# The feed-forward norm's list of work: turning a pair of tiles in the same step as the rounding of the pair before it

## The chip, the cores and the metric

The kernel runs on one core of a Trainium2 chip. The metric is the device time of one execution in microseconds; the times below are medians over runs.

## The reference, cut to what matters

The program computes two transformer blocks on 256 tokens of width 2048. The place of the change is the second half of the first block:

```
h = rmsnorm(x, norm_ffn_g) * (1.0 + scale_f) + shift_f
g, u = split(h @ ffn_w_in)              # 2048 x 2*5632
x = x + gate_f * ((silu(g) * u) @ ffn_w_down)
```

Everything is in float32. A product of float32 matrices is made of three products of rounded parts: weights and activations are each split into a rounded part (hi) and the rest (lo), and hi x hi, hi x lo and lo x hi are summed.

## The kernel before, in words

**Matrix products.** All weights stream from memory in chunks of two 128-row tiles (512 KB for a width of 512). SyncE loads a chunk into one of five raw buffers. ScalarE rounds it into a buffer of WHI (four of them), VectorE writes what is left into WLO, and TensorE then does the chunk's "unit": for both row tiles and both halves of the tokens three matmuls of 512 columns, twelve in all, with a tile of the activations standing in the array. A job is one output width of 512 over all of its chunks. The feed-forward's first job is fg 0, the second fu 0; each has eight units.

**The norm.** Before fg 0 the activations have to be normalized and turned, so that features lie on partitions. There are 16 feature tiles, handled as eight pairs. The parts are: `f_rn` (row sums, and the inverse root on GpSimd), `warm` (16 matmuls on constants), `f_sc` of a pair (VectorE scales the rows of X into XN), `f_T` of a pair (TensorE turns the pair, four transposes, into a PSUM bank; ScalarE multiplies and adds the modulation into hraw), `f_hi` of a pair (ScalarE rounds hraw into H's hi half; VectorE writes the rest into the lo half), and `f_gfb` (GpSimd loads a gain, once pair 7's rest is written). hraw has two places, one for even and one for odd pairs, so the scaling of pair n waits for the rest of pair n - 2. Unit n of fg 0 reads pair n. Each waits for its data by semaphores.

**What sets the order.** The order is made once, when the program is built: `make_timeline` (from line 417) makes one list, and each engine goes through this list and issues its own share of every entry, so the list is the order of every engine's queue. A stage such as "ffn" is a list of steps written out in `stage_steps` (lines 303 to 415). After every unit each running stage moves on by one step. Ahead of a unit, `until(*stat_need(...))` moves the stages on further until the steps that write this unit's pair and the next unit's are in the list (lines 464 to 471 say which step that is). "prep" entries, the conversion of a weight chunk, are put three units ahead of the unit that uses it. At fg 0, which is one of the BORDERS, the needed steps are put ahead of the "prep" of that moment. The stage "ffn" starts after the last unit of the output projection, xo 3.

The functions behind the parts: `f_T` for TensorE at line 1038, for ScalarE at 1551 with `norm_T` at 1376; `f_hi` at 1558 with `norm_hi` at 1387; VectorE's `f_sc` at 2250 and `f_hi` at 2256 with `norm_lo` at 1984; GpSimd's `f_gfb` at 2648. TensorE's `unit` (line 1203) asks `stationary` for pair n with

```
w.wait_ge(h_hi, at("h", s, k // 2))
w.wait_ge(h_lo, at("h", s, k // 2))
```

In rows of the trace, gp<-whi,h and gp<-wlo,h are a unit's matmuls, tp<-cst,xn a turning (line 833), hraw<-tp,modc ScalarE's scaling, h<-hraw its rounding, h<-hraw,h VectorE's rest, whi<-raw and wlo<-raw,whi a weight chunk's conversion, xn<-xs,stat the scaling of X.

Of the kernel before, what the change touches and what calls it, by code (L numbers as in the profile page):

```python
# [302 lines left out]
def stage_steps(sid):  # L303
# [3 lines left out]
    def step(*parts, need=()):  # L307
        return (list(parts), list(need))
# [23 lines left out]
    if kind == "gla":  # L332
        steps = [step(("gla_z", (), 0), ("gla_sc", (8, 0), 1), need=[("evac", "q", 1), ("evac", "k", 1)]), step(("gla_sc", (8, 1), 1))]
        steps += [step(("gla_sum", (p,), 1), need=[("gk", 5)]) for p in range(4)]
        steps += [step(("gla_diff", GLA_ORDER[0], 0)), step(("gla_exp", GLA_ORDER[0], 0))]
        for i, x in enumerate(GLA_ORDER):
            ahead = GLA_ORDER[i + 1:i + 2]
# [14 lines left out]
        (j,) = args  # L352
        return [idle, idle, idle, step(("mt_T", (j, 0), 1)), step(("mt_T", (j, 1), 1))]
    if kind == "ffn":
        steps = []
        for pair in range(8):
            first = [("f_rn", (), 0), ("warm", ("hf", 0), 1), *[("f_sc", (n,), 0) for n in range(4)]] if pair == 0 else []
            ahead = [("f_sc", (n,), 0) for n in (pair + 3, pair + 4) if pair in (1, 3)] + ([("f_gfb", (), 0)] if pair == 7 else [])
            steps += [step(*first, ("f_T", (pair,), 1)), step(*ahead, ("f_hi", (pair,), 0))]
        return steps  # L360
    if kind == "fx":
        (j,) = args
# [22 lines left out]
    if kind == "ret":  # L385
        l, which = args
        steps = []
# [8 lines left out]
    if kind == "diff":  # L396
        (l,) = args
        steps = []
# [5 lines left out]
    if kind == "lend":  # L404
# [3 lines left out]
        steps = []  # L408
# [8 lines left out]
def make_timeline(jobs, units, chunks):  # L417
# [6 lines left out]
    def launch(*sid):  # L424
        active.append([sid, 0, stage_steps(sid)])

    def step():
        for a in list(active):
            sid, i, steps = a
            parts, need = steps[i]  # L430
            if any(x not in done for x in need):
                continue
            for name, args, n in parts:
                got = []
                for _ in range(n):
                    b = rank[0] % 4
                    rank[0] += 1
                    got.append(Use(b, bank_n[b]))
                    bank_n[b] += 1
                uses[(name, *args)] = got  # L440
                line.append((name, args))
            done.add((*sid, i))
            a[1] += 1
            if a[1] == len(steps):
                done.add(sid)
                active.remove(a)
                if sid[0] == "adaf":
                    launch("fnorm", sid[1])
                if sid == ("fnorm", 2):
                    launch("tables")  # L450
                if sid[0] == "lx" and sid[2] == 1:
                    launch("lru", sid[1])
                if sid[0] == "lfirst":
                    done.add(("layer", 0))
                    launch("lres")
                if sid[0] == "lend" and sid[1] == 0:
                    done.add(("layer", 1))
# [8 lines left out]
    def stat_need(job, k):  # L466
        s = job["stat"]
        if s == "h":
            return [("fnorm", k // 4)]
        if s == "hf":  # L470
            return [("ffn", k // 2 * 2 + 1)]
        if s in ("lq", "lk"):
            return [("lat", s[1], 3 + k // 2)]
        if s == "ot":
            return [("pair", k // 2)]
        if s == "mt":
            return [("mt", k // 4, 3 + k % 4 // 2)]
        if s == "a":
            return [("fx", 6 * job["args"][0] + k // 4, 2 + k % 4 // 2)]
        if s == "h0":  # L480
            return [("hx", k // 4, 1 + k % 4 // 2)]
        if s == "h1":
            return [("lend", 0, k // 2)]
        if s == "mx":
            l = job["args"][0]
            if k < 6:
                return [("ret", l, k % 2, 12 + k // 2)]
            return [("diff", l, 10 * (k - 6) + 9)] if k < 10 else [("lg", l, (k - 10) // 3)]
        return []
# [3 lines left out]
    for n, (job, ci) in enumerate(units):  # L493

        if job["name"] in BORDERS and ci == 0:
            for k in job["order"][0:2]:
                for kk in range(job["kn"]):
                    until(*stat_need(job, k + kk))
# [13 lines left out]
        if job["kind"] != "ada":  # L512
# [15 lines left out]
            for k in job["order"][ci:ci + (1 if (job["name"], ci) == (("ymla", 0), 6) else 2)]:  # L528
                for kk in range(job["kn"]):
                    until(*stat_need(job, k + kk))  # L530
# [2223 lines left out]
```

## Time and profile before

| | us |
|---|---|
| median of 3 runs | 2645.58 |
| lowest, highest | 2645.3, 2647.14 |
| the profiled execution, its own time | 2647.02 |
| its span, first to last instruction | 2645.2 |
| busy: TensorE, VectorE, ScalarE, GpSimd | 2556.9, 1699.3, 1282.6, 63.3 |
| mean granted TensorE clock | 0.994 |

Busy time is a union of an engine's instructions, counted over the span. A row of the timeline gives the start, the duration, the engine, the line, the operation with what it writes and reads, how many were merged into it, and in brackets the idle time of the engine before it and what ended that. A merged row's duration covers all of its instructions. In the table by stretches a row gives, for each engine, the busy time and the number of instructions that started in it, and at the end TensorE's granted clock (1.00 is 2.4 GHz), the busy share of the DMA engines and their rate in GB/s.

### The profile page before, as it was taken

The page shows a single profiled execution, that of the slowest core. Times are in us where ns is not written, and L with a number is a line of the kernel's source. Part 1 is how long each engine was busy: PE and PEld are TensorE (multiplying, and loading weights), DVE is VectorE, ACT ScalarE, POOL GpSimd, SP SyncE. Part 2 cuts the span into 40 slices and gives each one's busy share as a digit, 9 for nine tenths or more (in the row PEclk, how much of TensorE's full clock was granted, in tenths as well). Part 3 has the DMA queues.
Part 4 walks back from the last instruction along what each step waited for, and adds up shares of the span by engine and source line. Part 5 has one row for each costly group of instructions (what it writes and reads, how often), then busy time and mean ns, then how long its engine had stood idle before and what let it go on. Part 6 is the DMA issues. An engine that isn't in the chain of part 4 may idle for free.

```text
span 2645.2 us, 33987 instructions
## 1 busy us (share of the span) xinstructions
PE 2556.9 (97%) x12327; PEld 2147.6 (81%) x12327; DVE 1699.3 (64%) x2194; ACT 1282.6 (48%) x1824; POOL 63.3 (2%) x102
## 2 busy tenths in 40 slices
PE   3889999999999999999999999999999999999999
PEld 3888887888887887788888888888888887988887
DVE  5887776776676755566655545565666655676664
ACT  3345455444555444544443444455755545565553
POOL 0000000000000000000000000000000100010000
PEclk9999999999999999999999999999999999999999
DMA  9984665888675765687756666556665465665564
GB/s 363 340 262 152 184 207 183 286 308 269 205 251 192 237 205 180 192 281 252 269 190 192 191 191 190 183 186 182 182 188 175 136 216 148 187 187 176 150 200 135
DMA packets 279921, 555.73 MB, mean 210 GB/s; under 512 B 24287, under 2 KB 45101, under 8 KB 279117
## 3 DMA queue, kind: packets, MB, share of 16 engines
q1 hardware_dynamic: 274048, 541.79, 64.6%
q0 software_dynamic: 3040, 8.69, 1.0%
q10 hardware_dynamic: 2668, 3.09, 0.3%
q8 instruction: 100, 1.64, 0.3%
q14 instruction: 65, 0.52, 0.1%
HBM read 549.83 MB, written 2.10 MB: 209 GB/s over the span
## 4 chain that ended last, share of the span: by engine, by line
PE 90%; DVE 4%; ACT 2%; issue 1%; DMA 1%; SPq 0%; POOL 0%; DVEq 0%; ACTq 0%
PE gp L830 83%; PE tp L830 5%; PE tp L833 2%; DMA raw_first<-in_ada_w_dram 1%; DVE wlo L1884 1%; ACT whi L1270 1%; DVE acc L1890 1%; DVE xs L1884 0%; ACT hraw L1270 0%; SPq L813 0%; DVE stat L2208 0%; ACT sx L1270 0%; DVE sx L1884 0%; DVE yd L1884 0%; ACT h L1270 0%
## 5 line engine op out<-in xcount | busy, mean ns | idle before, releaser
L1884 DVE TENSOR_TENSOR wlo<-raw,whi 128x1024 fp32r<-128x1024 f32 (+1 forms) x830 | 986.1, 1197 | 699.7 <-ACT whi L1270 697.1
L830 PE MATMUL gp<-whi,h 128*128 128x512 f32 (+1 forms) x4352 | 1373.2, 389 | 11.5 <-DVE h L1884 5.5
L1270 ACT ACTIVATE whi<-raw 128x1024 fp32r<-128x1024 f32 (+1 forms) x830 | 851.5, 1037 | 666.6 <-PE gp L830 537.3
L830 PEld LDWEIGHTS gp<-whi,h 128*128 128x128 f32 x4352 | 816.4, 188 | 171.5 <-issue 19.6
L830 PE MATMUL gp<-wlo,h 128*128 128x512 f32 (+1 forms) x2176 | 835.6, 384 | 0.0
L830 PEld LDWEIGHTS gp<-wlo,h 128*128 128x128 f32 x2176 | 410.4, 189 | 72.8 <-issue 1.7
L1890 DVE SCALAR_TENSOR_TENSOR acc<-raw,cact,acc 128x1024 f32<-128x1024 f32 x149 | 190.6, 1279 | 7.7 <-DMA raw<-in_ada_w_dram 7.0
L830 PE MATMUL gp<-whi,ah 128*128 128x512 f32 x352 | 138.0, 392 | 0.0
L830 PE MATMUL gp<-whi,al 128*128 128x512 f32 x352 | 137.1, 390 | 0.0
L830 PE MATMUL gp<-wlo,ah 128*128 128x512 f32 x352 | 137.0, 389 | 0.0
L830 PE MATMUL gp<-h,whi 128*128 128x256 f32 (+1 forms) x528 | 107.2, 300 | 20.7 <-ACT whi L1270 10.7
L830 PEld LDWEIGHTS gp<-h,whi 128*128 128x128 f32 (+1 forms) x528 | 88.5, 202 | 25.5 <-issue 15.9
L830 PE MATMUL gp<-whi,mxh 128*128 128x512 f32 x256 | 99.8, 390 | 0.0
L830 PE MATMUL gp<-whi,mxl 128*128 128x512 f32 x256 | 99.6, 389 | 0.0
L830 PE MATMUL gp<-wlo,mxh 128*128 128x512 f32 x256 | 99.6, 389 | 0.0
L830 PE MATMUL gp<-h,wlo 128*128 128x256 f32 (+1 forms) x272 | 79.8, 293 | 0.0
L830 PEld LDWEIGHTS gp<-whi,al 128*128 128x128 f32 x352 | 66.1, 188 | 13.9
L830 PEld LDWEIGHTS gp<-wlo,ah 128*128 128x128 f32 x352 | 66.1, 188 | 13.4
L830 PEld LDWEIGHTS gp<-whi,ah 128*128 128x128 f32 x352 | 66.1, 188 | 13.5
L2603 POOL TENSOR_TENSOR stat<-stat,cst 128x2 f32<-128x2 f32 (+1 forms) x37 | 30.2, 817 | 1436.9 <-DVE stat L1887 1436.8
L1270 ACT ACT_TABLE_LOAD x44 | 56.5, 1283 | 6.1 <-issue 2.8
L830 PEld LDWEIGHTS gp<-wlo,mxh 128*128 128x128 f32 x256 | 48.1, 188 | 10.0
(331 smaller groups left out, 2594.2 us busy)
## 6 DMA issues: line engine op xcount, KB each, us to landing
raw<-in_w_in_dram SPq DMA_DIRECT2D x310, 512.0 KB, 4.3
raw<-in_ffn_w_in_dram SPq DMA_DIRECT2D x176, 512.0 KB, 4.5
raw<-in_ada_w_dram SPq DMA_DIRECT2D x158, 512.0 KB, 5.0
raw<-in_w_out_dram SPq DMA_DIRECT2D x96, 512.0 KB, 4.4
raw<-in_ffn_w_down_dram SPq DMA_DIRECT2D x88, 512.0 KB, 4.4
raw<-in_w_in_dram SPq DMA_DIRECT2D x64, 384.0 KB, 3.5
raw_first<-in_ada_w_dram SPq DMA_DIRECT2D x34, 512.0 KB, 7.5
raw<-in_gla_wo_dram SPq DMA_DIRECT2D x32, 512.0 KB, 5.7
```

The costliest lines, as they stand in the source:

```text
L830: return e.matmul(o, l, r, start=start, stop=stop)
L833: return e.transpose(o, i, ident[0:n, 0:n])
L1270: return e.activation(o, i, f, **kw)
L1884: return e.tensor_tensor(o, a, b, op)
L1890: return e.scalar_tensor_tensor(out=o, in0=a, scalar=s, in1=b, op0=op0, op1=op1)
L2603: e.tensor_tensor(dst, dst, cst[:, C_HALF:C_HALF + n], ALU.pow).then_inc(pow_out, 1)
```

## The change

The diff has two hunks. The first writes out the steps of the stage "ffn": before, a pair was turned in one step and rounded in the next, 16 steps; now pair 0 is turned in a step of its own, and each of eight further steps rounds a pair and turns the next. In those steps the rounding stands first, then the turning of the next pair, then the scalings of later pairs (pairs 4 and 5 with pair 1, pairs 6 and 7 with pair 3). The second hunk says which step a unit's pair comes from.

```
     if kind == "ffn":
-        steps = []
+        steps = [step(("f_rn", (), 0), ("warm", ("hf", 0), 1), *[("f_sc", (n,), 0) for n in range(4)], ("f_T", (0,), 1))]
         for pair in range(8):
-            first = [("f_rn", (), 0), ("warm", ("hf", 0), 1), *[("f_sc", (n,), 0) for n in range(4)]] if pair == 0 else []
-            ahead = [("f_sc", (n,), 0) for n in (pair + 3, pair + 4) if pair in (1, 3)] + ([("f_gfb", (), 0)] if pair == 7 else [])
-            steps += [step(*first, ("f_T", (pair,), 1)), step(*ahead, ("f_hi", (pair,), 0))]
+            more = [("f_sc", (n,), 0) for n in (pair + 3, pair + 4) if pair in (1, 3)] + ([("f_gfb", (), 0)] if pair == 7 else [])
+            ahead = [("f_T", (pair + 1,), 1)] if pair < 7 else []
+            steps += [step(("f_hi", (pair,), 0), *ahead, *more)]
         return steps
...
         if s == "hf":
-            return [("ffn", k // 2 * 2 + 1)]
+            return [("ffn", k // 2 + 1)]
```

## Rows read from the trace of the kernel before

**Rows 1.** The page: TensorE's busy time; the chain of waits by engine and line

```profile
PE 2556.9 (97%) x12327; PEld 2147.6 (81%) x12327; DVE 1699.3 (64%) x2194; ACT 1282.6 (48%) x1824; POOL 63.3 (2%) x102
...
PE gp L830 83%; PE tp L830 5%; PE tp L833 2%; DMA raw_first<-in_ada_w_dram 1%; DVE wlo L1884 1%; ACT whi L1270 1%; DVE acc L1890 1%; DVE xs L1884 0%; ACT hraw L1270 0%; SPq L813 0%; DVE stat L2208 0%; ACT sx L1270 0%; DVE sx L1884 0%; DVE yd L1884 0%; ACT h L1270 0%
```

**Rows 2.** Stretches from unit to unit; columns as told above

```profile
1048.62:1050.31 1.69, 0.00 (x1) 0.00 (x1) 0.84 (x4) 0.00 (x0) 0.71 (x1) 1.00 0.04 16
1050.31:1051.49 1.18, 1.18 (x8) 0.84 (x8) 1.18 (x6) 0.41 (x1) 0.00 (x0) 1.00 0.00 0
1051.49:1053.64 2.15, 0.00 (x2) 0.03 (x1) 1.18 (x4) 2.12 (x5) 0.00 (x0) 1.00 0.00 0
1053.64:1058.05 4.41, 4.41 (x12) 3.44 (x13) 2.73 (x6) 1.62 (x3) 0.00 (x0) 0.61 0.13 15
1058.05:1058.41 0.36, 0.36 (x6) 0.36 (x4) 0.00 (x0) 0.00 (x0) 0.00 (x0) 1.00 0.36 46
1058.41:1062.86 4.45, 3.44 (x20) 2.68 (x18) 1.83 (x2) 3.46 (x7) 0.00 (x0) 1.00 0.27 103
1062.86:1082.01 19.15, 16.73 (x77) 12.85 (x77) 10.19 (x14) 12.37 (x20) 0.00 (x0) 1.00 0.48 137
1082.01:1084.73 2.72, 2.72 (x12) 2.28 (x13) 1.23 (x1) 1.42 (x2) 1.60 (x3) 1.00 0.81 265
...
1092.89:1713.00 620.11, 620.11 (x2772) 511.98 (x2770) 349.01 (x320) 257.15 (x269) 0.96 (x2) 1.00 0.69 216
```

**Rows 3.** Stretches at the norm ahead of layer 1

```profile
2212.37:2214.19 1.82, 0.00 (x0) 0.00 (x1) 0.98 (x4) 0.00 (x0) 0.71 (x1) 1.00 0.65 228
2214.19:2216.10 1.91, 1.77 (x8) 1.13 (x8) 1.01 (x3) 0.84 (x2) 0.00 (x0) 0.72 0.03 10
...
2216.85:2221.99 5.14, 5.14 (x12) 3.99 (x13) 3.19 (x5) 2.40 (x6) 0.00 (x0) 0.51 0.10 7
2221.99:2225.19 3.20, 3.20 (x17) 2.64 (x16) 1.55 (x3) 1.79 (x3) 0.00 (x0) 1.00 0.34 112
```

**Rows 4.** Timeline from pair 2's turning to its rest; last, scalings ahead of pair 3's rest

```profile
1058.82 1.02 ACT L1270 ACTIVATE hraw<-tp,modc 128x256 f32<-128x256 f32 x2 [3.52 <-issue]
...
1059.73 1.06 ACT L1270 ACTIVATE whi<-raw 128x1024 fp32r<-128x1024 f32 x1
...
1060.68 0.62 ACT L1270 ACTIVATE h<-hraw 128x512 fp32r<-128x512 f32 x1
...
1060.89 1.23 DVE L1884 TENSOR_TENSOR wlo<-raw,whi 128x1024 fp32r<-128x1024 f32 x1 [4.27 <-ACT whi L1270]
...
1062.03 0.68 DVE L1884 TENSOR_TENSOR h<-hraw,h 128x512 fp32r<-128x512 f32 x1
...
1065.10 1.14 DVE L1887 TENSOR_SCALAR xn<-xs,stat 128x256 f32<-128x256 f32 x4
```

**Rows 5.** Timeline ahead of unit 0: VectorE and ScalarE

```profile
1049.64 2.19 DVE L1887 TENSOR_SCALAR xn<-xs,stat 128x256 f32<-128x256 f32 x8 [0.84 <-POOL stat L2603]
...
1052.80 0.69 DVE L1884 TENSOR_TENSOR h<-hraw,h 128x512 fp32r<-128x512 f32 x1 [0.97 <-ACT h L1270]
...
1054.25 1.04 ACT L1270 ACTIVATE whi<-raw 128x1024 fp32r<-128x1024 f32 x1
```

**Rows 6.** The half microsecond before the granted clock falls

```profile
1054.00:1054.50 0.50, 0.50 (x4) 0.41 (x3) 0.50 (x4) 0.50 (x2) 0.00 (x0) 0.99 0.00 0
```

**Rows 7.** Stretches at an idle time in an early stage

```profile
263.00:264.80 1.80, 0.00 (x0) 0.00 (x0) 1.80 (x4) 0.21 (x1) 0.00 (x0) 1.00 0.12 10
264.80:266.00 1.20, 1.14 (x10) 1.15 (x11) 1.20 (x3) 0.00 (x0) 0.00 (x0) 1.00 0.81 215
266.00:269.30 3.30, 3.30 (x14) 2.91 (x13) 2.04 (x2) 3.12 (x4) 0.00 (x0) 0.50 0.47 141
```

**Rows 8.** DMA issues from 1040 to 1100: KB each, median us to landing

```profile
raw<-in_ffn_w_in_dram SPq DMA_DIRECT2D x14, 512.0 KB, 3.9
gfb<-in_final_norm_g_dram POOLq DMA_DIRECT2D x1, 1024.0 KB, 8.2
```

## The prediction

> **What bounds the kernel now.** I read the page first: TensorE is busy 97% of the span and its three lines hold 83, 5 and 2% of the chain of waits [rows 1]. Time is therefore gained only where TensorE stands still or runs slowly, and an edit counts only there. Next I cut the stage of the change into stretches, one per weight chunk ("unit": twelve matmuls of 512 columns), from the first matmul of one to that of another [rows 2]. In that table look at the length of a stretch against TensorE's busy time in it, and at the clock. The stage starts once the sums of squares are in (1048.62) and ends at 1084.73, where the job fg 0 is through and fu 0 begins; from 1092.89 on TensorE is busy for 620.11 of 620.11 us.
>
> Unit 1 with the turning behind it has 4.45, units 2 to 6 together 19.15, unit 7 2.72. What would a unit take if nothing were late? The turning between units 0 and 1 costs TensorE 0.36 (1058.05 to 1058.41) [rows 2]. The same twelve matmuls and a turning in the other norm of this kind, where nothing was late, took 3.20 (2221.99 to 2225.19) [rows 3]. So a unit with a turning costs 3.20, of which 2.84 are its own; unit 7, with none behind it, took 2.72 [rows 2]. Units 1 to 6, five with a turning and unit 6 without, would need 5 x 3.20 + 2.72 = 18.72; they have 23.60, and in the difference of 4.9 TensorE is idle.
>
> Why they are late is seen in one round [rows 4]. TensorE turns pair 2 at 1058.05. ScalarE scales it at 1058.82, converts a weight chunk at 1059.73 (the next thing in its list), rounds the pair at 1060.68; VectorE takes the chunk's rest at 1060.89 and the pair's rest at 1062.03, ending at 1062.71. Unit 2 starts 0.15 later. So 4.66 us pass from the turning to the pair being whole, and TensorE has only unit 1 (2.84) and the next turning to put there. For pair 3 VectorE also has four scalings ahead of the pair's rest, another 1.14 us [rows 4].
>
> **The change, part by part.** *The order.* Units need the same pairs as before, but a pair's rounding and the next pair's turning are one step. Worked through the list by hand: before, the list was T0, hi0, T1, hi1, chunk 3, unit 0, T2, chunk 4, hi2, unit 1, T3, chunk 5, hi3. After it is T0, hi0, T1, hi1, T2, chunk 3, unit 0, hi2, T3, chunk 4, unit 1, hi3, T4, chunk 5, unit 2. No instruction is added or removed: 32 transposes, 16 scalings of XN, 16 of hraw, 8 roundings, 8 rests. Each of T2 to T7 stands one unit earlier on TensorE.
>
> *T2 ahead of unit 0.* TensorE has nothing from 1051.49 to 1053.64, since unit 0 waits for pair 0's rest (1052.80 plus 0.69) [rows 2, 5]. T2 needs the sixth of the eight scalings, done by about 1049.64 + 6 x 0.27 = 1051.3 (0.27 is an eighth of their 2.19). It costs nothing there: 0.6 in a gap of 2.15. Were the gap gone it would cost its 0.36.
>
> *T2 and the chunk on ScalarE.* T2's two scalings (0.91 to the next start) now precede chunk 3, which started at 1054.25 [rows 5]. It starts at 1055.16 and is whole at about 1057.5; unit 3 wants it after 1063. Nothing on TensorE waits. The raw buffer behind it is freed 0.9 later; SP's load of the chunk five further on is issued so much later, and that chunk's conversion waits for unit 4 anyway. VectorE's four scalings for pairs 4 and 5 fall behind pair 1's rest: pair 1 is wanted only after unit 0.
>
> *A later round.* Pair 3 is turned right behind unit 0 in the place of pair 2. With the durations of [rows 4] (0.91, 0.95, then 0.62 on ScalarE, 1.14 and 0.69 on VectorE) it is whole 4.7 after that. It is wanted by unit 3, two units and two turnings later: 0.36 + 3.20 + 3.20 = 6.76. Slack 2.1. For pair 4 the four scalings stand behind the rest of pair 3 and not ahead of it, and have the same slack to go into. ScalarE needs 0.62 + 0.91 + 0.95 = 2.48 per unit and VectorE 1.14 + 0.69 + half of 1.14 = 2.40, both under 3.20. So the waits should all go, and the stage is TensorE's own time. Units 5 to 7 have no turning behind them now.
>
> *The sum without the clock.* From unit 0's start at 1053.64 to 1084.73 are 31.09. After: unit 0 with turning as before 4.77 (4.41 + 0.36), units 1 to 4 with turning 4 x 3.20 = 12.80, then 2.84 + 2.72 + 2.72 = 8.28; together 25.85. Gain 5.24: the 4.9 of waiting, and T2's 0.36, which now lies in a gap.
>
> *The clock.* Unit 0 took 4.41 and not 2.84 because the granted clock, full until 1054.5 [rows 6], has a mean of 0.61 in this stretch [rows 2]: it fell to the lower level, 1.2 in place of 2.4 GHz, 0.8 after unit 0 began and was back at the turning. What came before the fall: two idle times, 1.69 and 2.15, with 1.18 of turning between them. T2 takes about 0.5 off the second: 1.7 idle, 1.7 turning, 1.6 idle. Does the clock still fall? For a fall: elsewhere it fell 1.2 after a single idle time of 1.8 [rows 7], and before the norm of layer 1 it fell with 1.8 idle and then sparse transposes [rows 3]. Against: up to 1051.49 it had stood through an idle 1.69 and 1.18 of turning [rows 2]. Bounds: nothing, or 4.41 - 2.84 = 1.57. I take 1.57, since the piece that held (idle 1.69, turning) is nearest to the new second gap of 1.6 with more turning ahead of it; but it is close. Sum: 5.24 + 1.57 = 6.8.
>
> The Trainium skill (TensorE: Matmul & The Clock Gate, "Part 1: The HAM clock gate") says the gate's observation runs freely and doesn't begin with the kernel, so the same program meets it at another point each run. By that page neither outcome need hold in every execution, the gain would be 5.24 in some and 6.8 in others, and the fall in layer 1 could be shorter or longer after any shift; no single trace here can show it.
>
> That other fall can move for the same kernel time: it cost 5.14 for a first unit against 4.41 here, and 1.91 for the turnings against 1.18 [rows 2, 3], so 1.5 more. I allow 1.5 either way for it in the range.
>
> *Everything behind.* TensorE leaves the stage 6.8 earlier and is full afterwards. The loads: eight chunks of 0.52 MB and the 1.05 MB for GFB now in 24.3 us is 216 GB/s; from 1092.89 to 1713 the same rate, 216, went with a full TensorE [rows 2]. GFB's load took 8.2 us to land [rows 8] and is issued earlier by the gain and a bit more; its reader is the last norm of the block, far behind. Nothing is given back.
>
> **How it stands to the times.** The profiled execution took 2647.02 with a span of 2645.2; the median of three is 2645.58, 1.44 less. Taking 6.8 off gives 2640.2 for the profiled one and 2638.8 for the median, which I predict.
>
> **Rivals.** *A, forecast:* waits gone and clock held: 2638.8. Chance 0.46.
> *B: the clock falls all the same* at unit 0. 5.24 only: 2640.3, or down to 2638.9 if the other fall is the shorter one. For it: the falls of [rows 3, 7], after no longer idle times than are left here. Chance 0.37.
> *C: a new wait comes in.* The 4.7 of a round assumes that ScalarE is free when the turning ends; if each pair still ends late by half of today's excess, 2.6 remain: 2643.0. Against: slack of 2. Chance 0.08.
> *D: the change does nothing,* since the units' needs pull the steps forward and the list comes out nearly as before: 2645.6. Against: by hand the turnings do move. Chance 0.05.
> *E: slower.* Place: SP's ring of five raw buffers. It is emptied faster while GFB's load runs beside it. A chunk is loaded when its buffer's last rest is done and converted four units before use: five units of 2.72 less 2.3 for conversion and rest, 11 us later, with 8 more (three units) in converted chunks. It decides when a load lands after more than 19 us; price, each us beyond, and 5.24 + 5.3 have to be lost: 2651. Against: these loads land in 3.9 and GFB's own in 8.2 [rows 8]. Chance 0.04.
>
> **Numbers.** About 0.2% (5.3 us) is what a measurement of this kernel can tell from no change, and B's gain lies right at it. Faster: 0.46 x 0.9 + 0.37 x 0.55 = 0.62. Slower 0.04, the rest 0.34. Range: A and B with 1.5 for the other fall below A, up to nearly C above: 2636.8 to 2642.6; out are D, E and part of C.
>
> **What would show it.** In the profile after: T2 within 0.2 us of T1's end and before unit 0; unit starts 3.20 apart from unit 1 to unit 5, 2.7 to 2.8 after; no wait of TensorE for the rests of pairs 2 to 7; from unit 0 to fu 0 24.3 (A) or 25.9 (B); the clock row of unit 0 at 1.00 (A) or about 0.6 (B). Wrong if a unit after the first waits for a pair's or chunk's rest, or if the gain at fu 0 is lost by the end of the span.

## The result, and the profile after

| | us |
|---|---|
| changed kernel, median of 7 runs (lowest to highest) | 2637.97 (2635.92 to 2639.63) |
| kernel before, median of 7 runs beside it | 2646.16 (2642.69 to 2647.62) |
| ratio, 95% interval | 0.9969, 0.9957 to 0.998 |
| again, side by side: changed, median of 11 runs; before, median of 18 | 2639.19; 2645.67 |
| ratio, 95% interval | 0.9978, 0.997 to 0.9987 |
| profiled execution after: time, span | 2638.86, 2637.0 |

The kernel became faster by 0.2 to 0.3%, and both intervals lie below 1. In the two comparisons the medians differ by 8.2 and by 6.5 us; the trace says how much of it is the change's.

The changed kernel in stretches that correspond to those of [rows 2] (idle, turning, idle, unit 0, unit 1 with a turning, units 2 to 5, unit 7, and last the whole from unit 0 to fu 0):

```profile
1047.50:1049.19 1.69, 0.01 (x2) 0.01 (x1) 0.84 (x4) 0.00 (x0) 0.71 (x1) 1.00 0.02 8
1049.19:1050.90 1.71, 1.71 (x12) 1.25 (x12) 1.52 (x6) 0.94 (x2) 0.00 (x0) 1.00 0.00 0
1050.90:1052.52 1.62, 0.00 (x1) 0.03 (x1) 0.69 (x1) 1.59 (x4) 0.00 (x0) 1.00 0.00 0
1052.52:1055.37 2.85, 2.85 (x13) 2.28 (x14) 1.94 (x6) 2.82 (x6) 0.00 (x0) 1.00 0.00 0
1055.72:1058.93 3.21, 3.21 (x20) 2.64 (x18) 2.14 (x3) 2.48 (x4) 0.00 (x0) 1.00 0.38 105
1058.93:1071.37 12.44, 12.44 (x63) 10.27 (x62) 7.99 (x13) 9.95 (x16) 0.00 (x0) 1.00 0.57 163
1074.09:1076.81 2.72, 2.72 (x13) 2.25 (x12) 1.23 (x1) 2.34 (x2) 0.51 (x2) 1.00 1.03 383
1052.52:1076.81 24.29, 24.29 (x116) 20.05 (x117) 16.22 (x23) 18.88 (x29) 1.59 (x3) 1.00 0.51 156
```

The same whole of the kernel before:

```profile
1053.64:1084.73 31.09, 27.66 (x120) 21.62 (x121) 15.97 (x23) 18.88 (x29) 1.60 (x3) 0.95 0.43 125
```

Three pairs are now turned in one go of 1.71 us (two took 1.18), and the second idle time is 1.62 in place of 2.15. Unit 0 runs at a clock of 1.00 and takes 2.85 in place of 4.41. After it TensorE is busy in every stretch for all of its length: unit 1 takes 3.21 where it had 4.45. The two rows of the whole are the stage: 24.29 in place of 31.09, 6.80 less.

Where are the other 1.4 of the 8.2 us between the two spans (2645.2 and 2637.0)? The constant matmuls ended at 1047.50 in place of 1048.62, ahead of anything that the change touches: 1.12. The rest lies behind. First the changed kernel from fu 0 to layer 1's norm, in this norm up to its unit 1, and on to the end; then the same of the kernel before:

```profile
1076.81:2202.26 1125.45, 1123.92 (x5177) 938.14 (x5176) 666.87 (x792) 536.02 (x712) 20.65 (x31) 1.00 0.64 201
2202.26:2214.12 11.86, 9.15 (x34) 6.83 (x32) 7.41 (x16) 4.64 (x11) 0.71 (x1) 0.71 0.24 59
2214.12:2636.90 422.78, 415.69 (x2003) 351.11 (x2001) 261.59 (x415) 229.55 (x378) 20.30 (x29) 1.00 0.56 170
```

```profile
1084.73:2210.48 1125.75, 1124.21 (x5179) 938.24 (x5177) 667.08 (x792) 536.20 (x712) 20.67 (x31) 1.00 0.65 201
2210.48:2222.35 11.87, 9.15 (x34) 6.83 (x32) 7.40 (x16) 4.65 (x11) 0.71 (x1) 0.71 0.24 63
2222.35:2645.10 422.75, 415.66 (x2003) 351.08 (x2001) 261.57 (x415) 229.61 (x378) 20.35 (x29) 1.00 0.56 170
```

1125.45 and 1125.75, 11.86 and 11.87, 422.78 and 422.75: what was won in the stage is kept, and nothing else was won. In these two traces the change is worth 6.8 us; the other 1.4 lies where both kernels do the same, and is how two executions differ.

The timeline of the changed kernel shows a round, as [rows 4] did: the three turnings, pair 2's scaling and chunk 3, the turning of pair 3 behind unit 0, its scaling, chunk 4 on ScalarE and VectorE, the pair's rest, and unit 3.

```profile
1049.19 1.71 PE L833 MATMUL tp<-cst,xn 128*128 128x128 f32 x12 [1.68 <-DVE xn L1887]
...
1053.13 1.00 ACT L1270 ACTIVATE hraw<-tp,modc 128x256 f32<-128x256 f32 x2
...
1054.02 1.05 ACT L1270 ACTIVATE whi<-raw 128x1024 fp32r<-128x1024 f32 x1
...
1055.37 0.60 PE L833 MATMUL tp<-cst,xn 128*128 128x128 f32 x4
...
1056.00 1.02 ACT L1270 ACTIVATE hraw<-tp,modc 128x256 f32<-128x256 f32 x2 [0.41 <-PE tp L833]
...
1056.91 1.05 ACT L1270 ACTIVATE whi<-raw 128x1024 fp32r<-128x1024 f32 x1
...
1058.07 1.23 DVE L1884 TENSOR_TENSOR wlo<-raw,whi 128x1024 fp32r<-128x1024 f32 x1 [1.07 <-ACT whi L1270]
...
1059.21 0.68 DVE L1884 TENSOR_TENSOR h<-hraw,h 128x512 fp32r<-128x512 f32 x1
...
1062.12 0.48 PE L830 MATMUL gp<-whi,h 128*128 128x512 f32 x1
```

Pair 3 is turned at 1055.37 and its rest ends at 1059.89, 4.5 later, hardly shorter than the 4.66 of before. Unit 3 begins at 1062.12. The round (from the start of a pair's turning to the end of its rest) is nearly as long as it was; it now has 6.75 us to run in.

### The profile page after: what moved, and what is told of

The parts are those of the page before. It is cut to its first block, busy times and chain, and to the rows that moved or that the text cites. A ratio compares the mean times of both kernels' runs of the same rounds, so it can differ in the third digit from the quotient of the medians.

```text
span 2637.0 us, 33987 instructions
## 1 busy us (share of the span) xinstructions
PE 2552.6 (97%) x12327; PEld 2145.5 (81%) x12327; DVE 1699.4 (64%) x2194; ACT 1281.6 (49%) x1824; POOL 63.1 (2%) x102
## 4 chain that ended last, share of the span: by engine, by line
PE 91%; DVE 4%; ACT 2%; issue 1%; DMA 1%; SPq 0%; POOL 0%; DVEq 0%; ACTq 0%
PE gp L830 83%; PE tp L830 5%; PE tp L833 2%; DMA raw_first<-in_ada_w_dram 1%; DVE wlo L1884 1%; ACT whi L1270 1%; DVE acc L1890 1%; DVE xs L1884 0%; SPq L813 0%; ACT hraw L1270 0%; DVE stat L2208 0%; ACT sx L1270 0%; DVE sx L1884 0%; DVE yd L1884 0%; ACT h L1270 0%
```

## The experiments

All lengths below are from unit 0's first matmul to fu 0's, unless another is named: 31.09 before, 24.29 after. Each length is read from one profiled execution; e3, e5 and e8 were executed once and are read by their traces alone.

**e1: filling the idle time, nothing else.** On the kernel before:

```
-            steps += [step(*first, ("f_T", (pair,), 1)), step(*ahead, ("f_hi", (pair,), 0))]
+            fill = [("warm", ("hf", 1), 1)] if pair == 1 else []
+            steps += [step(*first, ("f_T", (pair,), 1), *fill), step(*ahead, ("f_hi", (pair,), 0))]
...
-            for n in range(4 if stat == "h1" else 8):
+            for n in range(4 if stat == "h1" else 2 if j == 1 else 8):
```

> The kernel before, with two more of the constant matmuls on TensorE between pair 1's turning and unit 0, where it stood idle for 2.15 us; nothing else moves. My theory: the gain of the change is two separate things, TensorE's waits for late pairs (4.9, and 0.36 for the turning that now lies in the gap) and the clock at unit 0 (1.57). Then here only the clock changes: unit 0's stretch 2.8 in place of 4.41, the waits ahead of units 2 to 7 stay, and from unit 0 to fu 0 it takes 31.09 - 1.57 = 29.5 us. Rival: it is not the length of the idle time that lets the clock fall, or one piece of work more doesn't hold it: 31.1, clock 0.6 in unit 0.

What is left of the idle time, unit 0, and the stage:

```profile
1051.75:1053.03 1.28, 0.00 (x1) 0.03 (x1) 0.84 (x2) 1.28 (x3) 0.00 (x0) 1.00 0.00 0
1053.03:1055.84 2.81, 2.81 (x12) 2.28 (x13) 2.56 (x6) 1.62 (x3) 0.00 (x0) 1.00 0.03 6
1053.03:1082.52 29.49, 26.06 (x120) 20.42 (x121) 15.96 (x23) 18.87 (x29) 1.60 (x3) 1.00 0.45 131
```

29.49, as the first theory had it. The 1.03 us of constant matmuls left 1.28 of idle time ahead of unit 0, unit 0 took 2.81 at full clock, and the waits stayed: TensorE is idle 3.4 of 29.49 in the row (29.49 less 26.06), as it was before (31.09 less 27.66). In time: 2643.62 against 2646.01, ratio 0.9992 (0.9983 to 1.0001), which alone would not settle it. The clock is one term, about 1.6, and work in the idle time is enough to get it, though no pair comes earlier.

**e2: pair 2 alone turned early.** On the kernel before:

```
-            steps += [step(*first, ("f_T", (pair,), 1)), step(*ahead, ("f_hi", (pair,), 0))]
+            turn = [("f_T", (pair,), 1)] if pair != 2 else []
+            more = [("f_T", (2,), 1)] if pair == 1 else []
+            steps += [step(*first, *turn), step(*ahead, ("f_hi", (pair,), 0), *more)]
```

> The kernel before, with pair 2's turning alone moved ahead of unit 0; pairs 3 to 7 stay behind units 1 to 5 as before. My theory: each late pair is its own round, so the clock holds (1.57), the turning is free (0.36) and only unit 2's wait goes (62.86 - 58.41 - 3.20 = 1.25): 31.09 - 3.18 = 27.9 us from unit 0 to fu 0, with the waits ahead of units 3 to 7 as before. Rival: the rounds hang on each other, and what is gained ahead of unit 2 is waited for again ahead of unit 3: 29.2. Second rival: one early pair is enough to bring all the others in time: 24.3.

Unit 0, from pair 3's turning to unit 3, and the stage; then from pair 3's turning to unit 3 in the kernel before:

```profile
1051.59:1054.43 2.84, 2.84 (x13) 2.37 (x14) 1.68 (x6) 2.54 (x5) 0.00 (x0) 1.00 0.02 6
1057.12:1062.85 5.73, 4.01 (x21) 3.06 (x20) 3.40 (x7) 4.05 (x7) 0.00 (x0) 1.00 0.64 181
1051.59:1080.59 29.00, 25.11 (x116) 20.01 (x117) 15.97 (x23) 18.89 (x29) 1.60 (x3) 1.00 0.46 132
```

```profile
1061.25:1066.98 5.73, 4.04 (x22) 3.05 (x20) 4.34 (x8) 3.13 (x7) 0.00 (x0) 1.00 0.43 104
```

29.00, and not 27.9: the rival that the next wait takes back what was won (29.2) is what happened. From the turning of pair 3 to unit 3 it is 5.73 in both kernels. In the kernel before, part of that round was spent in TensorE's wait for pair 2, which is why unit 3's own wait looked small. Of unit 2's 1.25 nothing stays won: 31.09 - 29.00 is 2.09, the clock and the free turning (1.57 + 0.36) and little else. The waits are not separate ones. One loop sets the pace, from a unit over the turning behind it and that pair's round to the unit two further on. In the kernel before, unit 3 starts at 1066.98, pair 5 is turned behind it at 1069.82, and unit 5, which needs pair 5, starts at 1074.50: a unit's 2.84 and 4.68 for the round and the start are 7.52 for two units. That reading was used for the expectation of e4b. In time: 2642.6, ratio 0.999 (0.998 to 1.0).

**e3: the new order with a falling clock.** On the changed kernel, half of the constant matmuls:

```
-            for n in range(4 if stat == "h1" else 8):
+            for n in range(4):
```

> The changed kernel with half as many constant matmuls ahead of the turnings, so that TensorE is idle 1.9 us longer before pair 0's turning. It is meant to make the clock fall with the new order. My theory: the two gains are independent, so that no unit waits for a pair, and the stage is longer by the slow stretch alone: 24.29 + 1.57 = 25.9, up to 26.7 if the clock falls before unit 0. Rival: with a slow unit 0 the later pairs come late again or the clock holds anyway (24.3).

Unit 0 and the stage:

```profile
1053.43:1058.16 4.73, 4.72 (x13) 3.68 (x14) 3.58 (x7) 3.05 (x6) 0.00 (x0) 0.57 0.01 3
1053.43:1079.60 26.17, 26.16 (x116) 21.45 (x117) 16.22 (x23) 18.89 (x29) 1.60 (x3) 0.92 0.48 146
```

26.17, within the expected 25.9 to 26.7. The clock had fallen already in the turnings (twelve transposes took 2.49 in place of 1.71) and was down for most of unit 0 (0.57 in the mean), which took 4.73, and in the row of the stage TensorE is busy for 26.16 of 26.17: no pair comes late though unit 0 is slow. This is the rival B of the prediction (25.85), brought about by an edit.

**e4, e4b: another cure for the same loop.** On the kernel before, the chunk's conversion put behind the next pair's rounding. The first attempt left out the second line:

```
-        if job["name"] in BORDERS and ci == 0:
+        if job["name"] in BORDERS and ci == 0 or job["name"] == ("fg", 0):
-            for k in job["order"][0:2]:
+            for k in job["order"][ci:ci + 2]:
```

> The kernel before with its sixteen steps and its turnings where they were; only the conversion of a weight chunk stands behind the rounding of the next pair in the list (for the eight units of fg 0), so that a round no longer has the chunk (0.95 on ScalarE, 1.14 on VectorE) in it. My theory: a late pair is the round's length of 4.66 against the 3.6 that TensorE has; without the chunk the round is 3.1 and the waits go although nothing is turned earlier: from unit 0 to fu 0 25.85 + 0.36 = 26.2, clock falling in unit 0 as before. Rival: what helps is the earlier turning, a unit's lead: 31.1, or partly, 28 to 29.

Without the second line the question is always for pairs 0 and 1, and the list comes out entry for entry as before. So e4 is the kernel before under another name:

```profile
1052.63:1083.70 31.07, 27.58 (x120) 21.57 (x121) 15.97 (x23) 18.88 (x29) 1.59 (x3) 0.95 0.42 122
```

31.07, and in time a ratio of 1.0002 (0.9993 to 1.0012): the repeat tells how well the stage's length stands (0.02) and how well the time does (0.1%).

> What the run with the chunk behind the pair was meant to be: its edit had asked for the same pairs at each unit and left the list as it was. Now pair n + 1's rounding stands ahead of the weight chunk's conversion at each unit of fg 0; turnings where they were before. The waits of the kernel before are a loop over every other unit: unit 3, the turning behind it, the round with the chunk in it, unit 5 (7.52 us from 1066.98 to 1074.50, and 7.51 to 1082.01, where two units of TensorE's own are 6.40). My theory: without the chunk the round is 3.1, the loop 5.9, and the waits go although no pair is turned earlier: 25.85 + 0.36 = 26.2 from unit 0 to fu 0 with the clock falling as before. Rival: a unit's lead of the turning is what is needed: 31.1, or 28 to 29 if only part goes.

With both lines. Unit 0 and the stage, then the round of pair 2 (turning, rounding, chunk, the pair's rest, the chunk's rest):

```profile
1052.40:1056.81 4.41, 4.41 (x12) 3.42 (x13) 2.73 (x6) 1.62 (x3) 0.00 (x0) 0.61 0.11 13
1052.40:1078.73 26.33, 26.33 (x120) 21.43 (x121) 16.43 (x23) 19.59 (x29) 1.60 (x3) 0.94 0.46 131
```

```profile
1056.81 0.60 PE L833 MATMUL tp<-cst,xn 128*128 128x128 f32 x4
...
1058.62 0.63 ACT L1270 ACTIVATE h<-hraw 128x512 fp32r<-128x512 f32 x1
...
1059.16 1.04 ACT L1270 ACTIVATE whi<-raw 128x1024 fp32r<-128x1024 f32 x1
1059.29 0.69 DVE L1884 TENSOR_TENSOR h<-hraw,h 128x512 fp32r<-128x512 f32 x1 [3.91 <-ACT h L1270]
...
1060.31 1.22 DVE L1884 TENSOR_TENSOR wlo<-raw,whi 128x1024 fp32r<-128x1024 f32 x1 [0.33 <-ACT whi L1270]
```

ScalarE's rounding (1058.62) now stands ahead of the chunk (1059.16), VectorE's rest (1059.29) ahead of the chunk's (1060.31), and the pair is whole 3.17 after its turning began, in place of 4.66. The stage takes 26.33 (expected 26.2), all of it busy, with the clock falling in unit 0 as before (4.41). That is 4.76 less than before. So the waits go without any pair being turned earlier: the rival that a lead is needed fell. In time: 2640.98, ratio 0.9984 (0.9975 to 0.9994).

**e5: the order within a step.** On the changed kernel:

```
-            steps += [step(("f_hi", (pair,), 0), *ahead, *more)]
+            steps += [step(*ahead, ("f_hi", (pair,), 0), *more)]
```

> The changed kernel with the order within a step turned round: the next pair's turning stands ahead of this pair's rounding. On ScalarE pair 1's scaling then stands ahead of pair 0's rounding, and later each rounding waits behind a scaling that waits for TensorE. My theory: unit 0 starts 1.0 later, and afterwards the slack of 2 takes the rest: from the end of the constant matmuls to fu 0 29.31 + 1.0 = 30.3 us, and 31.9 if the longer idle time lets the clock fall; no waits ahead of later units. Rival: the order within a step is of no account (29.3); second rival: the loop comes back through ScalarE and units 3 to 7 wait again (over 32).

From the end of the constant matmuls to unit 0, unit 0, and the stage:

```profile
1047.30:1053.08 5.78, 1.71 (x13) 1.29 (x13) 3.05 (x10) 2.48 (x6) 0.71 (x1) 0.99 0.01 5
1053.08:1057.47 4.39, 4.39 (x13) 3.45 (x14) 2.85 (x6) 2.46 (x4) 0.00 (x0) 0.62 0.01 4
1053.08:1078.91 25.83, 25.83 (x116) 21.22 (x117) 16.39 (x23) 18.71 (x28) 1.59 (x3) 0.94 0.47 141
```

5.78 against 5.02 (1.69 + 1.71 + 1.62): pair 0's rounding waits behind pair 1's scaling, and unit 0 starts 0.76 later (1.0 was expected). The longer idle time brought the clock down again, and unit 0 took 4.39. From the constant matmuls' end to fu 0 it is 31.6 (5.78 + 25.83; expected 31.9), 2.3 more than the changed kernel's 29.3. In this one execution the order inside the step costs a third of the gain, by way of the first pair and the clock; later units don't mind it (25.83 busy of 25.83).

**e6: one more unit of lead.** On the changed kernel:

```
-            ahead = [("f_T", (pair + 1,), 1)] if pair < 7 else []
+            ahead = [("f_T", (n,), 1) for n in ((2, 3) if pair == 1 else (pair + 1,) if pair < 1 else (pair + 2,)) if n < 8]
```

> The changed kernel with one more unit of lead: pair 3 too is turned ahead of unit 0, and pairs 4 to 7 one unit earlier than in the change. Theory: hraw has two places, so ScalarE's scaling of pair n waits for the rest of pair n - 2; with that scaling now ahead of the chunk in the list, scaling, chunk, rounding, chunk's rest and pair's rest become one loop of 0.91 + 0.95 + 1.14 + 0.69 and waits between, about 4.0 us a pair against 3.20. Pairs 4 to 7 come late again: 25 to 26.5 us from unit 0 to fu 0 in place of 24.29. Rival: more lead only helps, since pair 3's turning moves into the idle time: 23.9.

Units 4 and 5, and the stage; then the loop on ScalarE and VectorE:

```profile
1066.53:1070.45 3.92, 3.02 (x16) 2.18 (x14) 1.83 (x2) 2.39 (x5) 0.00 (x0) 1.00 0.46 134
1070.45:1074.46 4.01, 2.98 (x12) 2.17 (x13) 1.97 (x3) 4.01 (x7) 0.00 (x0) 1.00 0.47 131
1052.82:1080.00 27.18, 24.53 (x112) 19.42 (x113) 16.03 (x23) 18.70 (x29) 1.60 (x3) 1.00 0.45 130
```

```profile
1066.40 1.02 ACT L1270 ACTIVATE hraw<-tp,modc 128x256 f32<-128x256 f32 x2 [1.52 <-DVE h L1884]
...
1067.32 1.05 ACT L1270 ACTIVATE whi<-raw 128x1024 fp32r<-128x1024 f32 x1
...
1068.47 1.22 DVE L1884 TENSOR_TENSOR wlo<-raw,whi 128x1024 fp32r<-128x1024 f32 x1 [2.19 <-ACT whi L1270]
...
1069.62 0.68 DVE L1884 TENSOR_TENSOR h<-hraw,h 128x512 fp32r<-128x512 f32 x1
...
1070.42 1.02 ACT L1270 ACTIVATE hraw<-tp,modc 128x256 f32<-128x256 f32 x2 [1.53 <-DVE h L1884]
```

27.18: more than expected (25 to 26.5), but by the loop that was expected. The scaling at 1066.40 is followed by the chunk, the rounding, the chunk's rest and pair's rest, and the next scaling waits for this rest and starts at 1070.42, 4.02 later. TensorE falls to this pace (3.92 and 4.01). The estimate left out that the turning behind unit 2, too, had to wait, 0.72 for VectorE's late scalings of XN. The stage is 2.9 longer than the changed kernel's; the median is 2642.19, ratio 0.9986 (0.9977 to 0.9996). With two places of hraw and this order a lead of one unit is better than a lead of two.

**e8: both single cures on the kernel before** (the edits of e1 and e4b together).

> The kernel before with both of the single cures together: the chunk's conversion behind the pair's rounding, and two constant matmuls more in the idle time ahead of unit 0; no turning is moved. Theory: the terms add up, so that only the 0.36 of the turning which the change hides is missing: 24.29 + 0.36 = 24.65 us from unit 0 to fu 0. Rival: with a faster unit 0 the waits come back, over 25.5.

Unit 0 and the stage:

```profile
1053.96:1056.77 2.81, 2.81 (x13) 2.28 (x14) 2.56 (x6) 1.62 (x3) 0.00 (x0) 1.00 0.00 0
1053.96:1078.70 24.74, 24.74 (x120) 20.28 (x121) 16.42 (x23) 19.59 (x29) 1.60 (x3) 1.00 0.49 147
```

24.74, 24.65 expected. No turning was moved, and the stage is within 0.45 of the changed kernel's. The terms add up: waits, clock, and the one turning in the idle time.

**e7, e9: the same medicine for layer 1's norm, and the changed kernel again.** On the changed kernel, twice the constant matmuls there:

```
-            for n in range(4 if stat == "h1" else 8):
+            for n in range(8):
```

> The changed kernel with eight in place of four pairs of constant matmuls ahead of layer 1's norm, where TensorE is idle 1.8 us before its first turning and the clock falls (slow for two stretches as long as the one at unit 0 before the change). It asks whether what held the clock at unit 0 works there. Theory: the fall goes; the turnings take 1.2 in place of 1.9 and the first unit 2.85 in place of 5.1: 2.5 to 3 us less, 2635.3 in all and 0.1% under the changed kernel. Rival: the clock falls all the same after the second gap, ahead of the first unit: no gain, or up to 1; or the constant matmuls run into the time of the first turning and delay it by 0.1.

From the constant matmuls' start in layer 1's norm to unit 1, and unit 0 of it:

```profile
2202.64:2212.20 9.56, 8.12 (x41) 6.34 (x40) 7.28 (x16) 4.60 (x11) 0.71 (x1) 1.00 0.24 72
2209.00:2211.85 2.85, 2.85 (x13) 2.29 (x13) 2.73 (x5) 1.95 (x5) 0.00 (x0) 1.00 0.00 0
```

9.56 in place of 11.86, clock 1.00, unit 0 in 2.85: in the trace it does what was expected. But the median of six runs was 2637.32 where 2635.3 had been expected, and the ratio 0.997 (0.9959 to 0.9982) is no further from 1 than the changed kernel's in its first comparison. So both were run again side by side.

> The changed kernel as it is, for a tighter comparison beside the two below on one chip. By the trace the change itself is worth 6.8 us (31.09 to 24.29), while the first medians are 8.2 apart. Theory: the rest of the 8.2 is chance; 2638.5 to 2639.5 where the kernel before has 2645.5 to 2646, a ratio of 0.9974. Rival: something outside the stage gains too, 0.9969 again.

> The changed kernel with the longer constant work ahead of layer 1's norm, again, beside the changed kernel on the same chip. Its trace had the first unit there in 2.85 in place of 5.13 us, but its median (2637.32) was no better than the changed kernel's (2637.97) on another chip. Theory: the fall in that trace was a dear one, other executions lose half of it: 1 to 2 us under the changed kernel's median, and a narrower spread (1.1 us in six runs against 3.7 in seven). Rival: nothing is gained beyond the spread.

The stage and layer 1's norm of the changed kernel in the second run; then layer 1's norm in e8, which has the short constant work there and should have a fall too:

```profile
1053.53:1077.83 24.30, 24.30 (x116) 20.06 (x117) 16.20 (x23) 18.89 (x29) 1.60 (x3) 1.00 0.52 157
2203.21:2215.38 12.17, 9.00 (x33) 6.73 (x32) 7.40 (x16) 4.60 (x11) 0.71 (x1) 0.72 0.28 79
```

```profile
2204.41:2213.95 9.54, 6.37 (x33) 4.83 (x32) 7.25 (x16) 4.61 (x11) 0.71 (x1) 1.00 0.22 73
```

The stage is again 24.30. The changed kernel had 2639.19 in eleven runs, e9 2636.78 in eight; before 2645.67. The changed kernel's 6.5 with a ratio of 0.9978 (0.997 to 0.9987) has the traced 6.8 in it.

Why did the first comparison show 8.2? The times of both kernels fall into two groups with a gap between them. Of the 18 runs of the kernel before, eight lie at 2642.57 to 2643.12 with a mean clock of 0.996 and ten at 2645.39 to 2647.72 with 0.994; of the eleven of the changed kernel, two lie at 2635.54 and 2636.20 and nine at 2638.26 to 2640.64. Lower group against lower group the medians differ by 6.8, higher against higher by 7.0. In the first comparison one run of seven before and three of seven after were in the lower group, which drives the medians apart; in the second it was eight of 18 and two of eleven, which draws them together. So the 8.2 is in part the mix. No execution of the kernel before from its lower group was profiled. Which slow stretch is missing there, and whether it is ever the one at unit 0, stays open.

e9 is 2.4 below the changed kernel by the medians (1 to 2 had been expected), with a ratio of 0.9972 (0.9961 to 0.9982) to before; the two intervals overlap, so the times only make it likely that e9 is the better one. The traces don't settle it either. With the long constant work this norm took 9.56 in both profiles (e7 and e9) and the clock stayed at 1.00. With the short constant work it took 11.86 and 12.17 in the changed kernel's two profiles, but 9.54 in e8's, the last row above. The fall there is not the same in every execution, and two profiles without one don't show that the constant work took it away.

## Why the prediction was right

**What bounds it.** Right. The gain is TensorE's idle and slow time in one stage, and it is still there at the end of the span. One word of the reading is off: of the 4.9 lost from unit 1 to unit 6, [rows 2] show 3.4 as idle. Most of the rest lies behind the turnings: a turning's row is 0.60 long, where the next unit can follow after 0.36. As lost time the 4.9 is right.

**The order, worked.** Right: three turnings ahead of unit 0, each later one a unit earlier. Of T2 ahead of unit 0 it said 0.6 in a gap of 2.15; it took 0.53 (2.15 to 1.62).

**T2 and the chunk on ScalarE.** Chunk 3 began at 1054.02 with T2's scaling at 1053.13 ahead of it, 1.50 after unit 0's start where it had been 0.61. That is the 0.9 of the forecast, and nothing waited for it.

**A later round.** 4.7 forecast, 4.5 measured, wanted after 6.75: no wait. The step is right in its numbers. Where the reading was thin is in the picture behind it: the waits of before were taken as one per unit, a difference summed over units 1 to 6. e2 shows one loop over every other unit, in which a wait removed comes back at the next unit unless all later turnings move too. The sum didn't suffer, since the change moves all of them. That was luck rather than reasoning: the same reading, used for e2, missed by 1.1 (27.9 for 29.00). Nor was it said that the lead is only one of two cures; e4b removes the same waits by taking the chunk out of the round.

**The sum without the clock.** 25.85 forecast; e3 and e5, where the clock fell, have 26.17 (it fell already in the turnings) and 25.83 (with the order inside a step turned round). In the changed kernel itself, 31.09 less the 1.56 of the clock and less 24.29 is 5.24, the forecast term.

**The clock.** This was the open step, taken at 1.57 with "it is close" and with chances of 0.46 to 0.37. It held: 4.41 to 2.85. The reason given, one idle time of 1.69 that had done no harm, was thin, and the right side of a near-even choice is in part luck. Over all of the profiles here, the clock stood at unit 0 in the eight that have 1.62 or less of idle time ahead of it and 1.69 before the turnings (after twice, e1, e2, e6, e7, e8, e9), and fell in the four with 2.15 or more (before, e4, e4b, and e5 with 2.40). It fell as well in e3, with 3.41 before the turnings and only 0.84 ahead of unit 0: the last idle time alone doesn't decide. e1 against before is the clean pair, since nothing but work in the idle time differs. The Trainium skill (TensorE: Matmul & The Clock Gate, "Part 1: The HAM clock gate") was cited for the gate meeting the kernel at another point each run, by which neither outcome need hold every time. At unit 0 no profile shows that, though the lower group of the kernel before was never profiled; in layer 1's norm they do, 9.54 to 12.17 us with the same instructions. That the cause is the one the page gives, no run shows. The fall in layer 1 was put at 1.5 dearer than the one at unit 0, some 3.1 in all; the two norms of the changed kernel are 2.3 and 2.6 longer than the one without a fall.

**The sum.** 6.8 forecast, 6.80 in the trace, 8.2 and 6.5 by the two pairs of medians. The forecast of 2638.8 lies between 2637.97 and 2639.19. The range's lower end, 2636.8, is 2.0 below the forecast, though 1.5 was allowed there.

**Everything behind.** Right that nothing is given back. The rate it reckoned with, 216 GB/s in the stage, was 156, so the loads were under less strain than feared.

**Rivals.** B needs a falling clock and is e3. C's new wait didn't come; e6 shows that it does one unit further on. D falls by the timeline, where the turnings have moved; e4, whose list did not change, is what it would look like. E: GFB's load was issued at 1073.01, beside a stage that is all busy; the weight loads around it landed in 4.5 us and GFB's in 8.4, and no wait for a load is seen.

## What to carry to other kernels

When an in-order chain runs through several engines, measure the round (from the first step's start to the last's end) against the time that the bound engine can fill meanwhile, and look for what stands in the round without belonging to it: here a weight chunk's conversion. Starting every round earlier (the change) and taking the stranger out (e4b) cure the same waits. Starting a single one earlier (e2) doesn't, since the rounds hang on each other. And a lead beyond what the buffers between the engines can hold becomes a new wait (e6).

## What the runs showed of the hardware

An idle time of TensorE can cost more through the clock than by its length. 0.53 us of work moved into a gap of 2.15 let unit 0 take 2.85 in place of 4.41, 1.56 less. Work without any use (e1, 1.03 us of constant matmuls) does the same, 2.81.

The profiles differ in at least two places where the kernels do the same. The norm ahead of layer 1 took 9.54 to 12.17 us with the same (short) constant work. And the constant matmuls ahead of the stage, with the same work before them, ended between 1046.58 (e2) and 1049.50 (e9); what makes that difference stays open. The kernel before had 2641.52 to 2647.84 in 25 runs. The kernel of e7 and e9, whose two profiles have no fall in either norm, had 2636.66 to 2637.72 in six and 2636.05 to 2638.51 in eight.
